# Attention of a fused two-block layer: one loop over steps of probability blocks on every engine in place of a loop over groups

## The reference

```
logits = (jnp.einsum('bqhd,bkhd->bhqk', q_i, k).astype(jnp.float32) * scale
          + (F_i[..., :, None] - F[..., None, :]))
logits = jnp.where(k_pos[None, :] <= q_pos[:, None], logits, -jnp.inf)
p = jax.nn.softmax(logits, axis=-1).astype(v.dtype)
return jnp.einsum('bhqk,bkhd->bqhd', p, v)
```

## Time and profile before

| | |
|---|---|
| median of 3 runs | 3100.59 us (3097.95 to 3103.45) |
| the profiled execution | 3103.1 us |
| its span in the profile | 3101.4 us |
| attention core | 1548.8 to 2250.6 us of the span |
| PE busy, whole span | 2564.8 us (83%) |
| DVE, ACT, POOL busy | 1848.8, 1250.9, 563.9 us |

### The profile page before, as it was taken

How to read it: one execution, slowest core, us unless ns; L and a number is a source line. 1 busy time by engine, 2 the same in 40 slices (tenths; PEclk the granted TensorE clock), 3 DMA queues, 4 the chain that set the end, 5 groups by cost and what they waited for, 6 DMA issues and landing times. The chain is left out here.

```text
span 3101.4 us, 34604 instructions
## 1 busy us (share of the span) xinstructions
PE 2564.8 (83%) x12069; PEld 2116.0 (68%) x12069; DVE 1848.8 (60%) x2460; ACT 1250.9 (40%) x1817; POOL 563.9 (18%) x609
## 2 busy tenths in 40 slices
PE   3998767556999999981478888888685999999999
PEld 2766456455887888870377777777564888888887
DVE  6873693355888888875435555555445445554554
ACT  2212531105777777772245555555422121112111
POOL 1000020111111111104225555555400000000000
PEclk8999758757999999995599999999796999999999
DMA  5683233417968799985111110110042111111111
GB/s 210 220 291 111 96 122 102 158 42 304 393 269 318 289 390 399 398 326 217 55 52 42 41 35 31 41 31 32 7 176 68 41 54 54 41 54 41 54 54 55
DMA packets 137677, 443.01 MB, mean 143 GB/s; under 512 B 15134, under 2 KB 74050, under 8 KB 124264
## 3 DMA queue, kind: packets, MB, share of 16 engines
q1 hardware_dynamic: 124140, 394.97, 34.7%
q0 software_dynamic: 8144, 27.80, 2.5%
q10 hardware_dynamic: 5292, 18.94, 1.5%
HBM read 384.91 MB, written 56.76 MB: 142 GB/s over the span
## 5 line engine op out<-in xcount | busy, mean ns | idle before, releaser
L1622 PE MATMUL psum<-w_high,block_hT_high 128*128 128x512 f32 x576 | 233.4, 405 | 22.8 <-DVE w_low L1328 18.0
L2428 DVE TENSOR_TENSOR x<-x,psum 128x512 f32<-128x512 f32 x256 | 172.8, 685 | 112.4 <-PE psum L1624 112.4
L1622 PE MATMUL psum<-w_qkv_high,fox_hT_high 128*128 128x384 f32 x512 | 199.8, 390 | 34.5 <-DVE w_qkv_low L2118 25.0
L1623 PE MATMUL psum<-w_low,block_hT_high 128*128 128x512 f32 x576 | 226.7, 393 | 0.0
L1624 PE MATMUL psum<-w_high,block_hT_low 128*128 128x512 f32 x576 | 226.4, 393 | 0.0
L1328 DVE TENSOR_TENSOR w_low<-w_up,w_high 128x2048 fp32r<-128x2048 f32 x72 | 161.7, 2288 | 90.0 <-ACT w_high L1322 90.0
L1622 PE MATMUL psum<-hT_high,w_mlp_in_high 128*128 128x512 f32 x512 | 200.1, 391 | 7.1 <-DVE w_mlp_in_low L2405 7.1
L1623 PE MATMUL psum<-hT_low,w_mlp_in_high 128*128 128x512 f32 x512 | 199.9, 390 | 0.0
L1624 PE MATMUL psum<-hT_high,w_mlp_in_low 128*128 128x512 f32 x512 | 199.7, 390 | 0.0
L1622 PE MATMUL psum<-w_mlp_out_high,hiddenT_high 128*128 128x512 f32 x512 | 199.2, 389 | 0.0
L1623 PE MATMUL psum<-w_mlp_out_low,hiddenT_high 128*128 128x512 f32 x512 | 199.2, 389 | 0.0
(11 more groups left out here) (402 smaller groups left out, 6704.7 us busy)
## 6 DMA issues: line engine op xcount, KB each, us to landing
w_gate<-in_w_expert_gate SPq DMA_DIRECT2D x32, 2048.0 KB
w_up<-in_w_expert_up SPq DMA_DIRECT2D x32, 2048.0 KB, 9.1
w_down<-in_w_expert_down SPq DMA_DIRECT2D x32, 2048.0 KB, 10.4
v_aug<-in_w_ada SPq DMA_DIRECT2D x48, 512.0 KB, 4.8
expert_rows<-block_out ACTq DMA_DIRECT2D x36, 512.0 KB, 9.1
v_aug<-in_ada_w SPq DMA_DIRECT2D x32, 512.0 KB, 4.7
expert_rows<-work SPq DMA_DIRECT2D x1, 16384.0 KB, 44.1
w_mlp_in<-in_w_mlp_in SPq DMA_DIRECT2D x16, 1024.0 KB, 5.1
```

The costliest lines, as they stand in the source:

```text
L1622: pe.matmul(out, sh, mh, start=start, stop=False)
L1623: pe.matmul(out, sh, ml, start=False, stop=False)
L2428: dve.tensor_tensor(x3[:, t, at], x3[:, t, at], bank[4 + j % 4], ALU.add).then_inc(s_r, 1)
```

## The change

The loops over groups become loops over steps y from -20 to 159, one step for each block of probabilities. On PE a step is: turn the block of step y+1; make both logits of the group whose first block comes four steps later, if there is one; make the 3 or 4 products dealt to this step; weigh block y; turn a batch, if one is due. The 64 products of a pair are dealt over the first 18 of its 20 steps (c = y % 20), by number, across the ends of tiles. The other engines run the same steps, with the helpers in an order of their own. Buffers for probabilities grow from two to four (probs0 to probs3) and row sums from four to eight columns. Bank 7 is used in one place, so weigh of a group's first block waits for the emptying of the group before it. Blocks and batches get semaphores of their own (s_hi and s_lo, s_bh and s_bl). Both halves of the next weights are split in one step, c = 18.

```diff
-            pe_ = sbuf(c2, "probs_even", [P, 5 * P + 6 * P])
-            po_ = sbuf(c2, "probs_odd", [P, 7 * P + 8 * P])
+            pb = [sbuf(c2, f"probs{g}", [P, (4 * g + 3) * P]) for g in range(4)]
...
-            mn = sbuf(c2, "row_min", [P, 4])
-            rs = sbuf(c2, "row_sum", [P, 4])
+            mn = sbuf(c2, "row_min", [P, 8])
+            rs = sbuf(c2, "row_sum", [P, 8])
...
+            STEPS = 20
+            AHEAD = 4
+            BUSY = 18
+            blocks = [(n, b) for n in range(NG) for b in range(n % QUADS + 1)]
+            NY = len(blocks)
+            y_block = {nb: y for y, nb in enumerate(blocks)}
+            steps = range(-STEPS, NY)
 
...
+            def group_at(y):
+
+                n, b = blocks[y + AHEAD] if 0 <= y + AHEAD < NY else (None, 1)
+                return n if b == 0 else None
+
...
+            def products_at(y):
+
+                i, c = y // STEPS + 1, y % STEPS
+                if i >= PAIRS:
+                    return []
+                return [(TT * i + K // KT, K % KT) for K in range(KT * TT * c // BUSY, min(KT * TT, KT * TT * (c + 1) // BUSY))]
+
+            def tile_at(y):
+
+                done = [q for q, k in products_at(y) if k == KT - 1]
+                return done[0] if done else None
+
+            def batch_at(y):
+
+                q = tile_at(y) if y >= -STEPS else None
+                return q // 2 if q is not None and q % 2 == 1 else None
...
+                    for y in steps:
+                        if batch_at(y - 1) is not None:
+                            root(batch_at(y - 1))
+                        if group_at(y - 1) is not None:
                             for u in range(2):
-                                share(2 * (n + 1) + u)
+                                share(2 * group_at(y - 1) + u)
...
+                        if k == 0 and q >= 1:
+                            pe.wait_ge(s_raw, q)
+                            pe.wait_ge(s_vl, q)
+                        if k % 4 == 0:
+                            pe.wait_ge(s_wl, 2 * i + k // 4 + 1)
+                        ins = split_mm(pe, bank[4][:, 0:W3], (hTh[:, k, at], hTl[:, k, at]), (wh[:, k, :], wl[:, k, :]), k == 0, k == KT - 1)
+                        if k % 4 == 3:
+                            ins.then_inc(s_pj, 1)
...
+                    def bank_left(z):
+                        if z >= 2:
+                            kind, at = holds[z - 2]
+                            pe.wait_ge(s_hi if kind == "block" else s_bh, at + 1)
+                            pe.wait_ge(s_lo if kind == "block" else s_bl, at + 1)
+
                     def turn_probs(n, b):
                         i, h, g = where(n)
                         z = z_block[n, b]
-                        if z >= 2:
-                            pe.wait_ge(s_hi, z - 1)
-                            pe.wait_ge(s_lo, z - 1)
+                        bank_left(z)
                         if b == 0:
                             pe.wait_ge(s_p, 2 * n + 2)
...
+                        if b == 0 and n >= 1:
+                            pe.wait_ge(s_o, n)
+                        pe.wait_ge(s_lo, y + 1)
...
-                    for n in slots:
-                        logits(n + 1, 0)
-                        project(n, (0, 1))
-                        logits(n + 1, 1)
-                        project(n, (2, 3))
-                        if n >= 0:
-                            g = n % QUADS
-                            turn_probs(n, 0)
-                            project(n, (4,))
-                            for b in range(g + 1):
-                                if b < g:
-                                    turn_probs(n, b + 1)
-                                    project(n, (5 + b,))
-                                elif g < 3:
-                                    project(n, range(5 + g, KT))
-                                weigh(n, b)
-                        else:
-                            project(n, range(4, KT))
-                        if batch_in(n) is not None:
-                            turn_batch(batch_in(n))
+                    for y in steps:
+                        if 0 <= y + 1 < NY:
+                            turn_probs(*blocks[y + 1])
+                        if group_at(y) is not None:
+                            logits(group_at(y), 0)
+                            logits(group_at(y), 1)
+                        for q, k in products_at(y):
+                            project(q, k)
+                        if y >= 0:
+                            weigh(*blocks[y])
+                        if batch_at(y - 2) is not None:
+                            turn_batch(batch_at(y - 2))
...
-                    for n in slots:
-                        if batch_in(n - 1) is not None:
-                            high_batch(batch_in(n - 1))
-                        if n >= 1:
-                            copy_out(n - 1)
-                        if 0 <= n + 1 < NG:
-                            exp(2 * n + 2)
-                        if n >= 0:
-                            high_probs(n, 0)
-                        if n % TT == TT - 1 and n // TT + 2 < PAIRS:
-                            high_weights(2 * (n // TT + 2))
-                        if 0 <= n + 1 < NG:
-                            exp(2 * n + 3)
-                        if n >= 0:
-                            for b in range(1, n % QUADS + 1):
-                                high_probs(n, b)
-                        if n + TT < NT:
-                            rows_out(n)
-                            if n % 2 == 1:
-                                square((n + 7) // 2)
-                        if n % TT == TT - 1 and n // TT + 2 < PAIRS:
-                            high_weights(2 * (n // TT + 2) + 1)
+                    for y in steps:
+                        if 0 <= y + 1 < NY:
+                            high_probs(*blocks[y + 1])
+                        if left_at(y) is not None:
+                            copy_out(left_at(y))
+                        if group_at(y - 1) is not None:
+                            exp(2 * group_at(y - 1))
+                            exp(2 * group_at(y - 1) + 1)
+                        if batch_at(y - 3) is not None:
+                            high_batch(batch_at(y - 3))
+                        if y % STEPS == BUSY and y // STEPS + 2 < PAIRS:
+                            high_weights(2 * (y // STEPS + 2))
+                            high_weights(2 * (y // STEPS + 2) + 1)
+                        if tile_at(y) is not None:
+                            rows_out(tile_at(y))
+                        if batch_at(y) is not None:
+                            square(batch_at(y))
...
-                    for n in slots:
-                        if 0 <= n + 1 < NG:
-                            forgotten(2 * n + 2)
-                        if batch_in(n - 1) is not None:
-                            low_batch(batch_in(n - 1))
-                        if n >= 1:
-                            add_out(n - 1)
-                        if batch_in(n) is not None:
-                            sums(batch_in(n))
-                        if n >= 0:
-                            low_probs(n, 0)
-                        if n % TT == TT - 1 and n // TT + 2 < PAIRS:
-                            low_weights(2 * (n // TT + 2))
-                        if 0 <= n + 1 < NG:
-                            forgotten(2 * n + 3)
-                        if batch_in(n) is not None:
-                            normed(batch_in(n))
-                        if n >= 0:
-                            for b in range(1, n % QUADS + 1):
-                                low_probs(n, b)
-                        if n + TT < NT:
-                            v_low(n)
-                        if n % TT == TT - 1 and n // TT + 2 < PAIRS:
-                            low_weights(2 * (n // TT + 2) + 1)
+                    for y in steps:
+                        if 0 <= y + 1 < NY:
+                            low_probs(*blocks[y + 1])
+                        if left_at(y) is not None:
+                            add_out(left_at(y))
+                        if batch_at(y - 2) is not None:
+                            normed(batch_at(y - 2))
+                        if group_at(y) is not None:
+                            forgotten(2 * group_at(y))
+                            forgotten(2 * group_at(y) + 1)
+                        if batch_at(y - 1) is not None:
+                            sums(batch_at(y - 1))
+                        if batch_at(y - 3) is not None:
+                            low_batch(batch_at(y - 3))
+                        if y % STEPS == BUSY and y // STEPS + 2 < PAIRS:
+                            low_weights(2 * (y // STEPS + 2))
+                            low_weights(2 * (y // STEPS + 2) + 1)
+                        if tile_at(y) is not None:
+                            v_low(tile_at(y))
```

## The result

| | before | with the change |
|---|---|---|
| median of the runs | 3099.27 us (3092.22 to 3103.45, 4 runs) | 3330.85 us (3324.29 to 3331.79, 4 runs) |
| ratio, 95% interval | | 1.0745 (1.0721 to 1.077) |
| the profiled execution | 3103.1 us, span 3101.4 | 3330.23 us, span 3328.5 |
| attention core | 701.8 us | 927.9 us |

The account below looks back on a forecast made before the run. PE sets the pace but waits, mainly for probsT_low. Opening 82, six periods 654, seventh 97 and last pair 61 give 894 us against 701.8, +192: 3295 from the profiled execution's 3103.1, 3293 as median; range 3205 to 3370.

Parts of the forecast that it names:

- rival A: The forecast itself: in-order queues make PE wait longer than before; 3240 to 3345 us, periods of 102 to 116; 77 in 100.
- six periods: Attention core, each attending one pair and projecting the next: 66 us of PE work plus 41 stalls plus 2 clock, 109 each.
- seventh period: Attention core, the period with no weights to split: 97 us.
- last pair: End of the attention core, no batches, tiles or weights: 61 us with clock, against 72.6 before.
- clock in a period: Seven stalls per period each bring a stretch at 1.2 GHz, mostly covered by the next stall: 2 us added.
- Point 1: Weights at c = 18: both halves in a row through one buffer, with reload, stall PE 13.2 us.
- Point 2: Batches at c = 7, 16 and 0: copied out too late for a following turn, stalls 3.3, 2.8 and 5.5 us.
- Point 3: Tiles ending inside steps c = 2, 4, 11, 13: next products wait for rows_out and v_low, 1.9, 1.4, 5.6, 3.9 us.
- Point 4: POOL: shares of g = 3 late for the turn at c = 5, 2.7 us; a batch's root late at c = 10, 0.9.
- B: Delayed engines catch up, so tile and batch waits halve and weights remain: period 95, 3195 us; 8 in 100.
- C: The whole stage runs at a lower clock: a period 12 to 15 us more, about 3380 us; 10 in 100.
- D: Faster: low parts ahead of time are all that matters, four blocks of lead cover the stalls; 3007 us; 5 in 100.

Follow-up runs that it names:

- Experiments 1 to 3: Changed kernel with one edit each: weight halves apart, 3282.77 us; tiles always ending with their step, 3280.83 us; batch copies first in ACT's and DVE's steps, 3295.61 us.
- Experiment 4: Kernel before, with both weight halves split in a row at the end of a pair's last slot on ACT and DVE: 3150.1 us, ratio 1.0146.
- Experiment 9: Changed kernel with weight halves apart, whole tiles, batch copies before blocks, logits five blocks ahead, and bank 7 emptied first in each step: 3063.57 us, 0.9859 to before.
- experiments 1 and 5: Changed kernel with weight halves apart alone, 3282.77 us; and with weight halves apart, whole tiles and batch copies first together, 3244.43 us.
- Experiment 8: Kernel before, with PE alone turning a group's first block after the first logits and products between turn and weigh: 3127.23 us, ratio 1.0075.
- experiment 10: Experiment 9 with DVE's batch sums ahead of the forgotten rows and its first weight half split one step later, at c = 19: 3064.77 us.

## Why the prediction came out as it did

The likeliest case, rival A, held: in-order queues make PE wait longer than before. The changed kernel ran 38 us above the number and inside A's own range. Two misses of a period partly cancel, a clock term that was too small and stalls that were a little too large. By terms:

| term | predicted | measured |
|---|---|---|
| opening to the end of step 0 | 82 | 83.2 |
| six periods | 654 (109 each) | 674.6 (112.4 each) |
| seventh period | 97 | 105.2 |
| last pair | 61 | 64.9 |
| stage | 894 | 927.9 |
| stalls in a period, pause ends included | 41.2 | some 38 (36.1 idle, 1.8 of ends) |
| clock in a period | +2 | about +9 |

**The stalls, points 1 to 4: right in place and order, a little too large.** Point 1 was 13.2 us and is 11.60. From DVE's end at 1950.24 to ACT's next start at 1955.01 the reload takes 4.77 us, where the earlier trace rows gave 5.05. The 3.8 us that the prediction worked out from the Trainium skill's "DMA: Bandwidth & Descriptors" are an estimate for another path and lie 1.0 under the row. Point 2 was 5.5, 3.3 and 2.8 and is 4.54, 2.57 and 2.62. Point 3 was 12.8 and is 10.9, with 5.49 at c = 11 for 5.6. Point 4 was 3.6 (2.7 and 0.9) and is 3.9: 2.92, 0.16, and 0.77 at a turn that I hadn't listed. Experiments 1 to 3 each removed most of the waits that the point names (56 of 84, 59 of 86 and 65 of 71 us). Experiment 4 reproduced the price of point 1 in the other kernel, where the wait is one of products for the weights.

**The clock: the term that was mis-sized.** I took +2 us per period, since the next stall would cover the slower work. In the middle window PE is busy 8.7 us longer than in the earlier trace rows for the same number of matmuls within two, at 0.83 of the clock for 1.00. Experiment 9 runs as many in nearly the same order on PE at 0.96 and is back at 67 to 68 us. So it is the clock and not the order that makes PE's work longer. The rows after a stall show it: a turn of three takes 0.87 us at 1969.01, where a turn of four took 0.63, and the first product after the 5.49 takes 0.66. In windows of 2 us over the period the clock is at its lower level (0.50 of full) in six stretches, each in or just behind one of the stalls of 2.57 us or more; the 3.12 us at c = 13 brought none. So the prediction's count of seven was nearly right, and what failed is that the next stall covers the slower work. In the kernel before it was covered: a period of 81.7 or 81.8 us held PE busy 67.80 us at 1.00 of the clock or 71.81 at 0.94. That it is not here has a likely reason, which I only argue: the engine for which PE waits begins each step with PE's own, late turn. A period so comes out 3.4 us above its 109, 6.7 more for the clock and 3.3 less for the stalls. That is 20.6 us over six; the seventh adds 8.2, the last pair 3.9 and the opening 1.2, together the 34 that the stage is over its sum (the rest of the 38 lies outside the stage and between the medians and the profiled executions). The Trainium skill's "TensorE: Matmul & The Clock Gate", section "Terms", prices the throttle as the time at the lower level times one minus the ratio of the levels. By the granted clock of 0.83 a third of the period, 38 us, is at the lower level. By that rule 19 us would be lost, an estimate. The trace shows 8.7, less than half of it: a good part of the low time lies in the waits themselves, 8.5 us of it in the wait of 11.60 alone (at 0.50 from 1951 until PE starts at 1959.49).

**The seventh period** was to save the 12 us that a period with weights pays, and saved 7. Its wait for the scaled rows is 2.2 us for 11.8, but the waits for POOL are 6.1 for 3.7 and outT is 1.9 for none. Like experiments 1 and 5 it shows one wait less and part of it back.

**What the prediction priced at nothing.** The weigh that waits for the group before was given 0, "0 to 0.5 us". In the changed kernel that is right for the six periods, and wrong for the last pair: of 12.8 us in the stage, 1.9 lie in the seventh period and 10.9 in the last pair, in seven waits of up to 1.9. And it is right in this order only: with the batch ahead of it the wait is 49 us, with the other two edits as well 84, and experiment 9 takes most of it away (11.0 are left) by the place of the emptying in a step. POOL was larger than its 3.6 us per period suggest, 60 to 101 us by the lead alone.

**The rivals.** B, stalls half as large because engines catch up, is refuted: all ten stalls are within 1.6 us of their price, and only the smallest (0.9, now 0.16) is halved. C, the clock, was half right: PE's busy time rose, but a period is 3.4 us longer than 109, where C had 12 to 15. D, faster, is refuted for this order. Experiment 9, 1.4% faster than before with its wait for low parts gone, suggests that D's premise is worth something once the other queues are in order; that this wait is what pays is not shown by itself. Experiment 8 moved the turns in the old order and made it 0.75% slower. What is left open: whether a second buffer for the weights would take the reload away in this order, and how much bank 7 in two halves would give in the new order. The second wasn't tried, since PE would write one half while ACT and DVE read the other with nothing that orders them.

## What to carry to other kernels

When every engine's queue is dealt into steps, count for each handover how many steps the producer's queue holds ahead of it: here one more block of lead for the logits was worth 60 to 101 us, and the place in a step at which bank 7 is emptied 79. A stall that is taken away uncovers those behind it (133 us of single gains gave 86 together), so the gain of an edit is to be read in a kernel in which the others are made too. Price idle time of TensorE twice, once as the wait, and once in the slower matmuls after it. The second price varies: over the stage of the changed kernel 184 us more idle time came with 43 us more busy time, and in experiment 4 26 us came with 25.

## What the runs showed of the hardware

An operation of POOL took longer beside a weight split of DVE. In experiments 9 and 10 POOL's scaling of the sums (128 x 8) takes 1.63 and 0.20 us. In experiment 9 DVE splits the low weights, from two operands in SBUF, at the same time (start, us):

```profile
1919.73 1.75 DVE L2130 TENSOR_TENSOR w_qkv_low<-w_qkv,w_qkv_high 128x1536 fp32r<-128x1536 f32 x1
```

```profile
1919.90 1.63 POOL L1936 TENSOR_SCALAR qk_sums<-qk_sums 128x8 f32<-128x8 f32 x1 [1.03 <-DVE qk_sums L2167]
...
1923.90 1.89 POOL L1945 TENSOR_SCALAR probs<-probs,row_sum 128x640 f32<-128x640 f32 x1
```

In experiment 10 the split starts at 1925.98, and another operation of POOL meets it:

```profile
1923.39 0.20 POOL L1936 TENSOR_SCALAR qk_sums<-qk_sums 128x8 f32<-128x8 f32 x1
...
1925.95 3.46 POOL L1945 TENSOR_SCALAR probs<-probs,row_sum 128x640 f32<-128x640 f32 x1
```

The share of 640 columns takes 3.46 us for 1.89: 1.57 longer, nearly the split's 1.75. The same two durations return at six loads of experiment 9 (1.63) and at seven of experiment 10 (3.46). At 1923.39 the small operation took its 0.20 us beside DVE's forgotten rows (1923.30 to 1924.25), which read one operand from PSUM. The Trainium skill, "SBUF — State Buffer", section "Who interferes with whom", says that a DVE instruction with two inputs in SBUF and a GpSimd instruction that reads SBUF exclude each other. The trace agrees for the split: in both cases POOL's operation is longer by about what is left of DVE's. It shows no such thing for a short instruction of this kind: at 1925.37 DVE scaled a batch's rows for 0.69 us, and POOL's operation from 1925.30 kept its usual 0.55. So the place of a weight split in DVE's queue moves POOL's chain too: in the changed kernel a row-sum operation of POOL that mostly takes 0.57 us took 1.67 at 1948.97, beside the split of 1948.48. Whether experiment 10 lost some of its gain there, no run tells.
